# A hybrid decoder step on one core: norm and weight parts between the residual adds, down sums one group ahead, GpSimd issuing the down weights' transfers

## The reference, cut to what matters

```python
def out_and_mlp(x, a, b, w_out, g_mlp, w_up, w_down):
    x = x + jnp.concatenate([a, b], axis=-1) @ w_out
    hn = rmsnorm(x, g_mlp)
    return x + jnp.square(jax.nn.relu(hn @ w_up)) @ w_down

# per layer (one layer here), for x_prompt (1024 rows) and x_sample (8 x 8 rows), D_MODEL = 1024, D_FF = 4096
q, k, v, qi, ki, wi, bg, cg, h = project(rmsnorm(x, g_mix), w_in)
a = prompt_attention(...) or sample_attention(...)     # top-256 keys per query, 8 heads x 64
b, conv = conv_mixer(bg, cg, h, prev, conv_w)          # bg * conv3(cg * h), 512 channels
x = out_and_mlp(x, a, b, w_out, g_mlp, w_up, w_down)
y = rmsnorm(x, g_final)
```

## Time and profile before

| | us |
|---|---|
| median of 3 runs | 1790.15 (1788.7 to 1791.39) |
| the profiled execution, its time | 1778.85 |
| its span, first to last instruction | 1777.0 |
| PE busy | 1644.1, 93% |
| DVE busy | 997.3, 56% |
| ACT busy | 830.0, 47% |
| GpSimd busy | 628.2, 35% |
| mean granted PE clock | 0.955 of full speed |

### The profile page before, as it was taken

The page is one execution under the profiler, slowest core; times in us unless marked ns, Lnnn a source line. Parts: engine busy times, 40 slices in busy tenths (PEclk is TensorE's granted clock), DMA queues, the critical chain, the costliest instruction groups (busy, mean ns, idle before and its releaser), DMA issues.

```text
span 1777.0 us, 27949 instructions
## 1 busy us (share of the span) xinstructions
PE 1644.1 (93%) x10208; PEld 1267.5 (71%) x10208; DVE 997.3 (56%) x2212; ACT 830.0 (47%) x1597; POOL 628.2 (35%) x839
## 2 busy tenths in 40 slices
PE   8999999999888887778799879999999899999996
PEld 6653554999755565555579878888888788888885
DVE  5587889995634444444455764544444354444445
ACT  5565877775244444333353234444444353333334
POOL 1101325475645555544413214445445300400002
PEclk9999999999989989888999969999999999999998
DMA  8211320155867765554661136666666695455553
GB/s 242 52 48 52 119 68 36 46 173 174 268 206 222 218 191 162 156 154 135 185 168 36 36 112 208 217 222 205 218 224 224 222 337 166 162 188 172 163 172 134
DMA packets 153366, 288.47 MB, mean 162 GB/s; under 512 B 16971, under 2 KB 65471, under 8 KB 150930
## 3 DMA queue, kind: packets, MB, share of 16 engines
q1 hardware_dynamic: 131858, 214.97, 36.7%
q0 software_dynamic: 21376, 71.75, 13.5%
HBM read 215.18 MB, written 71.48 MB: 161 GB/s over the span
## 4 chain that ended last, share of the span: by engine, by line
PE 65%; issue 11%; DVE 8%; another core or an unknown queue 5%; ACT 5%; DMA 3%; POOL 2%; SPq 0%; DVEq 0%; POOLq 0%; ACTq 0%
PE psum L2407 6%; PE psum L2408 6%; PE psum L2409 6%; PE psum L2492 5%; PE psum L2494 5%; PE psum L2493 5%; PE psum L2235 2%; PE psum L2115 2%; PE psum L2257 2%; PE psum L1914 2%; PE psum L2144 2%; PE psum L1957 2%; PE psum L1958 1%; PE psum L1959 1%
## 5 line engine op out<-in xcount | busy, mean ns | idle before, releaser
L3269 DVE TENSOR_TENSOR ring_lo<-arena,ring_hi 128x1024 fp32r<-128x1024 f32 x112 | 141.3, 1264 | 159.5 <-ACT ring_hi L1653 159.3
L1653 ACT ACTIVATE ring_hi<-arena 128x1024 fp32r<-128x1024 f32 x112 | 118.6, 1060 | 194.2 <-DMA arena<-h_scratch 194.2
L2492 PE MATMUL psum<-ring_hi 128*128 128x512 f32 x448 | 176.7, 394 | 5.5 <-DVE ring_lo L3269 4.2
L2494 PE MATMUL psum<-ring_hi,ring_lo 128*128 128x512 f32 x448 | 175.5, 392 | 0.0
L2493 PE MATMUL psum<-ring_lo,ring_hi 128*128 128x512 f32 x448 | 175.0, 391 | 0.0
L1480 ACT ACTIVATE arena<-x_region,arena 128x384 bf16<-128x384 f32 (+2 forms) x192 | 166.5, 872 | 6.2 <-POOL arena L1192 6.2
L1227 POOL DMA_INDIRECT arena<-in_cache_v,arena x128 | 126.5, 988 | 112.6 <-PE psum L2216 79.4
L2630 DVE TENSOR_TENSOR wu_lo<-arena,wu_hi 128x512 fp32r<-128x512 f32 x112 | 83.7, 774 | 99.9 <-ACT wu_hi L1646 79.7
L1227 POOL DMA_INDIRECT arena<-in_cache_k,arena x96 | 96.4, 1004 | 100.8 <-PE psum L2115 77.2
L1545 ACT ACTIVATE arena<-psum 128x512 f32<-128x512 f32 (+3 forms) x64 | 33.2, 518 | 208.4 <-remote 104.2
L1646 ACT ACTIVATE wu_hi<-arena 128x512 fp32r<-128x512 f32 x112 | 67.9, 625 | 122.9 <-PE psum L2427 94.4
(11 more groups left out here) (429 smaller groups left out, 4081.3 us busy)
## 6 DMA issues: line engine op xcount, KB each, us to landing
h_scratch<-arena SPq DMA_DIRECT2D x112, 256.0 KB, 2.4
arena<-h_scratch SPq DMA_DIRECT2D x112, 256.0 KB, 3.6
arena<-in_w_down SPq DMA_DIRECT2D x16, 1024.0 KB
s_scratch<-arena SPq DMA_DIRECT2D x16, 1024.0 KB
arena<-s_scratch SPq DMA_DIRECT2D x64, 256.0 KB, 3.3
arena<-in_w_up SPq DMA_DIRECT2D x30, 512.0 KB, 4.4
arena<-in_w_down SPq DMA_DIRECT2D x48, 256.0 KB, 2.8
arena<-k_scratch SPq DMA_DIRECT2D x32, 256.0 KB
```

The costliest lines, as they stand in the source:

```text
L1653: act.activation(ring_hi[s % RING], ring_full[s % RING], ACT.Copy).then_inc(dn_high, 1)
L2492: pe.matmul(out, w_hi[:, col], h_hi, start=first, stop=False, skip_group_check=True)
L2494: ins = pe.matmul(out, w_lo[:, col], h_hi, start=False, stop=(k == NG - 1), skip_group_check=True)
L3269: dve.tensor_tensor(ring_lo[s % RING], ring_full[s % RING], ring_hi[s % RING], ALU.subtract).then_inc(dn_low, 1)
```

## The change

- DVE's `norm`, `low_early` and `low_late` are cut into pieces (`norm_root`, `norm_rows`, `norm_t3`, `norm_t2`, `norm_t1`, `low_n`, `low_t1`, `low_t2`, `low_t4`) that stand one behind each residual add u = 8 to 22, with the `up_low(0, i)` spread over u = 13 to 15. ACT's order follows: `norm_high(0)` ahead of the weight roundings.
- The third chunk's norm and parts are split in finer steps with more semaphore counts (`norm_high_last`, `low_last`), and its reciprocal and rows stand ahead of the first bank sums.
- In pass v = 1 the products go in the order 0, 4, 1, 2, 3, 5, 6, and sample half 0 follows product 2; in v = 0 `rms(2)` follows the second product.
- Sample half 0 uses one matmul of 256 columns for weights 0 and 2 together.
- `raw_down` and `sums_down` are issued by GpSimd. `down_sums(0)` comes before the group loop, and the sums of group g are made in the iteration that makes the up sums of group g, one group earlier than before.
- Ring slots 3, 4 and 5 lie in other places, and `fill(3)` to `fill(5)` stand before `h_sums`.
- The second halves of the last four row tiles are scaled by ACT instead of GpSimd.

```diff
-FIRST_NO = {i: n for n, i in enumerate((0, 2, 4, 1, 3, 5, 6))}
+UP_ORDER = {0: (0, 2, 4, 1, 3, 5, 6), 1: (0, 4, 1, 2, 3, 5, 6)}
...
+        wu_pair = at("wu_pair", w_at[0], 2048, F32R).rearrange("p (e x k c) -> p e x k c", e=2, x=2, k=4)
+        for e, i in enumerate((0, 2)):
+            wu_hi[i], wu_lo[i] = wu_pair[:, e, 0], wu_pair[:, e, 1]
...
-        ring_at = [RAWAT, WBLK, WBLK + 2048, WBLK + 4096, T4LO, T4HI]
+        ring_at = [RAWAT, WBLK, WBLK + 2048, T4LO, T4HI, WBLK + 4096]
...
@@ sync @@
-            raw_down(0)
             for g in range(NG):
...
-                    sums_down(g - 1)
-                    raw_down(g)
...
-                    sums_down(g)
                 h_second(v, g)
                 if g == NG - 1:
                     sp.wait_ge(up_done, up_no(v, 4))
                     fill(2)
+                    sp.wait_ge(up_done, 7 * len(VG))
+                    fill(3)
+                    sp.wait_ge(us_done, 2 * NG)
+                    fill(4)
+                    fill(5)
                 h_sums(v, g)
-            sp.wait_ge(us_done, 2 * NG)
-            fill(3)
-            sp.wait_ge(up_done, 7 * len(VG))
-            fill(4)
-            fill(5)
...
@@ gpsimd @@
+            def raw_down(k):
+                if k:
+                    pool.wait_ge(stg_out, STG_OUT0 + 16 * k)
+                pool.dma_start(stg, w_dn_v[:, 2 * k:2 * k + 2, :]).then_inc(stg_in, 16)
...
-            for g in range(NG):
-                if g + 1 < NG:
-                    for x in (1, 2, 3, 4):
-                        up_sum(g + 1, x)
-                    pool.wait_ge(w_low, weight_no(g + 1, 6))
+            pool.wait_ge(wo_ready, 3 * KT)
+            raw_down(0)
+            down_sums(0)
+            sums_down(0)
+            for g in range(1, NG):
+                for x in (1, 2, 3, 4):
+                    up_sum(g, x)
+                    if x == 1:
+                        raw_down(g)
+                pool.wait_ge(w_low, weight_no(g, 6))
                 down_sums(g)
+                sums_down(g)
...
-            for t in range(NB):
+            for t in range(NB // 2):
                 pool.wait_ge(row_scaled, ROW_SCALED0 + t + 1)
...
@@ scalar @@
             squares(1, 0, 4)
-            for i in (0, 2, 1, 4, 5, 3, 6):
+            norm_high(0)
+            squares(1, 4, 5)
+            for i in (0, 2, 1, 4):
                 up_high(0, i)
-            squares(1, 4, 5)
-            norm_high(0)
-            squares(1, 5, KT)
+            squares(1, 5, 6)
+            for i in (5, 3, 6):
+                up_high(0, i)
+            squares(1, 6, KT)
...
+            for t in range(NB // 2, NB):
+                act.wait_ge(row_scaled, ROW_SCALED0 + t + 1)
+                act.activation(yrow[t][:, 512:1024], yrow[t][:, 512:1024], ACT.Copy, scale=yroot[:, t:t + 1]).then_inc(y_rows_act, 1)
...
@@ tensor @@
+                    if half == 0:
+                        both = bank(7)[:, 0:2 * P].rearrange("p (e c) -> p e c", e=2)
+                        pe.matmul(both, n_pair[:, k, :], wu_pair[:, :, 0, k, :], start=(k == 0), stop=False, skip_group_check=True)
+                        ins = pe.matmul(both[0:SMP], n_pair[:, k, SMP:P], wu_pair[:, :, 1, k, :], start=False, stop=False, skip_group_check=True)
+                        continue
...
@@ vector @@
-                if u == KT + 1:
-                    norm(0)
-                if u == KT + 4:
-                    low_early(0)
-                if u == KT + 5:
-                    for i in (0, 2, 1, 4, 5, 3, 6):
-                        up_low(0, i)
...
+                if u == 8:
+                    norm_root(0)
+                if u == 9:
+                    norm_rows(0, 0, 6)
+                if u == 10:
+                    norm_rows(0, 6, KT)
+                    norm_t3(0)
+                    norm_t2(0)
+                if u == 11:
+                    norm_t1(0)
+                if u == 12:
+                    low_n(0)
+                if u == 13:
+                    low_t1(0)
+                    up_low(0, 0)
+                    up_low(0, 2)
...
+            norm_root(2)
+            norm_rows(2, 0, KT)
             first_sums(0)
             add_bank(0, 2, 4, h22, h22)
-            norm(2)
-            norm_t4(2)
-            dve.tensor_tensor(two_id, ident[:, 0:SMP], ident[:, SMP:P], ALU.add)
+            norm_t3(2)
+            norm_t2(2)
+            norm_t1(2)
             low_last()
```

More of the change, by code:

```diff
@@ L837, in up_no @@
         def up_no(v, i):
-            return 7 * v + (i if v else FIRST_NO[i]) + 1
+            return 7 * v + UP_ORDER.get(v, range(7)).index(i) + 1
         def weight_no(g, i):
@@ L1730, in _ @@
             h_from_bank(0)
-            norm_high(2)
+            norm_high_last()
             t4_high(2)
@@ L2393, in up_product @@
                 if v == 1:
[L2394 to L2395 removed]
+                    pe.wait_ge(n_low, {0: 5, 4: 5, 1: 6, 2: 6, 6: 9}.get(i, 7))
+                    if i == 4:
+                        pe.wait_ge(up_dve, 1)
+                    if i in (0, 4, 1, 2):
                         pe.wait_ge(wo_done, 3 * KT)
@@ L2418, in up_sample @@
                 if half and g == 0:
-                    pe.wait_ge(n_low, 8)
+                    pe.wait_ge(n_low, 10)
                 for k in range(4):
[L2421 to L2426, removed]
+                    if half == 0:
[3 more added lines that the diff above has]
+                        continue
+                    for e, w, s_pair in ((0, 3, n_pair[:, 4 + k, :]), (1, 6, sd_pair[:, k, :])):
+                        pe.matmul(bank(7)[:, e * P:(e + 1) * P], s_pair, wu_hi[w][:, k, :], start=False, stop=False, skip_group_check=True)
+                    for e, w, s_pair in ((0, 3, n_pair[:, 4 + k, :]), (1, 6, sd_pair[:, k, :])):
                         ins = pe.matmul(bank(7)[0:SMP, e * P:(e + 1) * P], s_pair[:, SMP:P], wu_lo[w][:, k, :],
-                                        start=False, stop=(half + k == 4), skip_group_check=True)
+                                        start=False, stop=(k == 3), skip_group_check=True)
                 ins.then_inc(us_done, 1)
@@ L2441, in _ @@
                 end = v == LASTV[g]
[L2442 to L2450, removed]
+                order = UP_ORDER.get(v, range(7))
+                for n, i in enumerate(order):
+                    up_product(v, i)
+                    if v == 0 and n == 1:
+                        rms(2)
+                    if g and n == 0:
                         turn_sample_h(g - 1)
-                    up_product(v, 1)
-                    up_product(v, 2)
-                    if end:
+                    if end and n == (3 if v == 1 else 2):
                         up_sample(g, 0)
-                    for i in (3, 4, 5, 6):
-                        up_product(v, i)
                 if end:
@@ L2555, in link, with norm_root, norm_rows, norm_t3 @@
                 dve.wait_ge(dve_step, steps[0] + steps[1])
-            def norm(c):
-                o, w = CH[c]
-                lo, hi = PAIRS[c]
+            def norm_root(c):
+                w = CH[c][1]
                 dve.wait_ge(root_ready, c + 1)
                 link(dve.reciprocal(root[:, 0:w], root[:, 0:w]))
-                for k in range(KT):
+            def norm_rows(c, first, last):
+                o, w = CH[c]
+                for k in range(first, last):
                     i = dve.scalar_tensor_tensor(out=n_full[:, k, o:o + w], in0=xT[:, k, o:o + w], scalar=colsT[:, KT + k:KT + k + 1],
                                                  in1=root[:, 0:w], op0=ALU.mult, op1=ALU.mult)
-                i.then_inc(norm_ready, 1)
-                dve.wait_ge(norm_ready, c + 1)
-                even, odd, into = halves(n_full, lo, hi, 0), halves(n_full, lo, hi, 1), halves(xT, lo, hi, 1)
-                link(dve.tensor_tensor(odd[:, 0:4], odd[:, 4:8], odd[:, 0:4], ALU.subtract))
-                dve.wait_ge(x_out, X_OUT0 + 16 * (c + 1))
-                link(dve.tensor_tensor(into[:, 4:8], odd[:, 0:4], even[:, 0:4], ALU.add))
-                dve.tensor_tensor(into[:, 0:4], odd[:, 4:8], into[:, 4:8], ALU.subtract).then_inc(n_made, 1)
+                if last == KT:
+                    i.then_inc(norm_ready, 1)
+            def norm_t3(c):
+                lo, hi = PAIRS[c]
+                odd = halves(n_full, lo, hi, 1)
+                dve.wait_ge(norm_ready, c + 1)
+                i = dve.tensor_tensor(odd[:, 0:4], odd[:, 4:8], odd[:, 0:4], ALU.subtract)
+                if c == 2:
+                    i.then_inc(n_made, 1)
+                    dve.wait_ge(n_made, 3)
+                else:
+                    link(i)
+            def norm_t2(c):
+                lo, hi = PAIRS[c]
+                dve.wait_ge(x_out, X_OUT0 + 16 * (c + 1))
+                link(dve.tensor_tensor(halves(xT, lo, hi, 1)[:, 4:8], halves(n_full, lo, hi, 1)[:, 0:4], halves(n_full, lo, hi, 0)[:, 0:4], ALU.add))
+            def norm_t1(c):
```

(3 more changed lines are left out.)

103 lines of the change are left out of this document (70 added, 33 removed).

## The result

The changed kernel takes 1809.35 us (1800.97 to 1815.0, 4 runs) where the kernel before took 1789.43 (1783.32 to 1791.39) beside it: ratio 1.0113, 95% interval 1.0064 to 1.0162. It is 20 us slower; 8.4 faster was forecast.

The account below looks back on a forecast made before the run. TensorE, busy 93%, bounds the kernel through its waits and half clock. 13.2 - 12.8 + 7.0 + 1.0 = 8.4 us off the median 1790.15 gives 1781.7 us; own range 1770 to 1793, eight in ten 1759 to 1803.

Parts of the forecast that it names:

- The place and the wait: Steady groups: up sum 2 waits in GpSimd's queue for the landed write, delaying ACT, DVE's bank sum and product 6; 2.0 us later.
- the sum of the round: Steady groups: 23.9 us a round against PE's 22.4, binding in 12 of 14 groups; stage 12.8 us longer, sample gain included.
- The round without meetings: Steady groups: bank sum to write 16.27, then 3.84, 0.54, 1.62 and 1.39 us, together 23.7 us a round.
- The meetings of DVE and GpSimd: Steady groups: up sum 3 takes turns with DVE's two low parts, adding 0 to 2 x 1.3 us; 0.2 taken.
- slower rival: Steady groups: DVE and GpSimd meet twice each round, 26.3 us a round, stage 41 us longer, 1810 us; chance 0.25.
- The first part: First residual add to v = 2: stall before the second root sum goes, v = 1 stays at half clock; gain 13.2 us.
- The meeting of DVE and the first down sums: Before v = 1: GpSimd's four first down sums lengthen DVE's chain by 0 to 5.2 us, 4.5 taken.
- The sample pairing: Sample half 0: eight matmuls of 256 columns for sixteen of 128 gain 0.37 us in each of 15 groups, 5.6 us.
- The start of the down products: First down products: earlier fills, last write and read out of SyncE's way, remove waits and half clock; gain 7.0 us.
- The last rows: End of kernel: ACT scales four of GpSimd's eight row halves; gain 1.0 us, 0 to 1.7.
- The clock holds: Rival: pass v = 1 keeps full clock, the rest as forecast, 1769.4 us; chance 0.13.

Follow-up runs that it names:

- the late read: Changed kernel with GpSimd issuing the read of the next down weights behind up sum 4 instead of up sum 1: 1746.36 us against 1776.38 before, ratio 0.9822.
- the run in which up sum 3 waits: Changed kernel with one wait added, up sum 3 starting only after DVE's low part of weight 1: 1778.57 us, ratio 1.0013 to the kernel before.
- the old scheme: Changed kernel with the down weights wholly as before (SyncE issues, down sums a group later), other edits kept: 1763.84 us against 1784.76 before, ratio 0.9875.

## Why the prediction was wrong, point by point

**The place and the wait: right.** Up sum 2 behind the wait for the landed write, ACT, DVE and the bank sum behind it, PE's product 6 last; the loop of five hand-overs; all of it is in the rows, and moving the read by one place removes it.

**The step that failed is the sum of the round, 23.9 us.** Two terms were mis-sized.

- *The round without meetings*, forecast at 23.7, measured at 24.53. From write to read 4.45 where 3.84 of SyncE's row was taken: 0.6. The sentence on the Trainium skill (DMA: Bandwidth & Descriptors, "Anatomy of one DMA — SWDGE (gpsimd) path") had 4.4, and this trace agrees: 4.43 and 4.45 from issue to the next instruction, the landing itself 4.2 behind the issue in the median. The read's issue 0.75 for 0.54: 0.2. Up sum 2 and the low parts 2.62 for 3.01: -0.4. The chain from bank sum to write 16.72 for 16.27: 0.45. Together 0.9. About 0.2 of it belongs to the added wait of the run that it is read from, so that 24.3 is nearer the truth.
- *The meetings of DVE and GpSimd*, forecast at 0.2, measured at 0.82 (one) and 1.87 (two). I had bounded them by 0 and 2.6 and put the value near the lower end, since a late PE would hold up sum 3 back. The rows show why it mostly doesn't: the wait moves up sum 2 so far back that product 4 is done when it ends, so up sum 3 follows at once (1251.40) and meets the low part of weight 2 in 11 of 13 rounds. A late PE holds back up sum 4 (0.47 us in the round from 1192.98, 0.21 in that from 1244.97), which is the difference between the two kinds of round. What I had counted on, a PE late enough to hold up sum 3, came in the two rounds behind 6.8 us of half clock, and there the low part of weight 1 took 1.79 instead.

Against PE's own 22.30 this makes 2.2 us a round and, on average, 1.2 more. Of the 14 rounds from the second write to the last, one takes 25.90 us on average in the changed kernel (1064.17 to 1426.82) and 22.47 in the late read: 48 us, where the forecast had 12 x 1.5 + 0.4 = 18.4. The stage: 335.2 + 47.3 = 382.5. By the run in which up sum 3 waits, 30.6 of the 47.3 are the queue's wait and 16.7 the meetings; with the 0.2 us a round that its own wait adds, nearer 28 and 19. So the slower rival's time (1810) came true, and its mechanism in part: its 26.3 us counted two meetings on 23.7; it is one or two meetings on 24.3 to 24.5.

**The first part: right, 12.7 for 13.2.** The stall ahead of the second root sum is gone with its half clock (1.00 from 980 to 1000), and from the first residual add to the first up product it is 93.5 us instead of 100.9, 7.4 less (7.0 forecast). From there to v = 1 it took 21.0 us, as forecast, but made up otherwise: PE waited 1.13 us at the root sum, for GpSimd's sum of squares, and 1.61 us before product 5, for the bank sums that stand behind the norm rows now (0 and 0 forecast), and 2.43 instead of 5.3 before v = 1. That these add up to the forecast is luck. The meeting of DVE and the first down sums was sized right: four operations took 4.1 us longer (1.68, 1.66, 2.29, 1.76), 4.5 forecast. The pass v = 1 took 23.1 us (22.3) at clock 0.51, with a wait of 1.16 us before product 6 that the forecast did not have.

**The sample pairing: right**, 0.45 for 0.37 a group; a matmul of 256 columns doesn't cost what two of 128 do. **The start of the down products: right in size** (6.7 for 7.0), and of the causes named the last write in SyncE's queue did most of it (5.6 of 8.7 us between the old scheme and the late read; the rest is open), the places of the fills nothing. **The last rows: right**, 1.0; that GpSimd's longer drain would else have cost 1.7 was not foreseen.

**The clock holds: refuted.** I had named two conditions, that the down sums miss DVE's chain and that PE's short waits don't cost the clock. With the first one given, the clock held for 8.5 us and then fell at a wait of 1.91 us for ACT, which half clock had hidden until then: the second condition failed.

## What to carry to other kernels

A DMA that waits for an earlier one to land belongs in the queue of an engine that has nothing urgent behind it, or behind the last urgent instruction; write down what follows it in the queue and where that engine waits anyway, since a wait that overlaps an existing one is free (0.85 us here) and the same wait one place earlier cost 47 us. When a wait moves an instruction, ask which others it now coincides with: a bound that looked unlikely in the old timing can become the rule in the new one (11 of 13 rounds here). A stall behind which a queue is already late is a loop: price the whole round, not the one delay.

## What the runs showed of the hardware

DVE's low parts, with both inputs in SBUF, took 1.7 us beside a GpSimd sum instead of 0.69 (that of weight 0, off the bounding chain, up to 2.3), while GpSimd's own took 1.29 and 1.47; DVE's bank sums, with one input in PSUM, kept their time beside GpSimd's sums. In the late read:

```profile
1217.26 1.29 POOL L1297 TENSOR_TENSOR arena<-arena 128x512 f32<-128x512 f32 x1
1218.62 1.28 POOL L1299 TENSOR_TENSOR arena<-arena 128x512 f32<-128x512 f32 x1
...
1218.06 0.69 DVE L3334 TENSOR_TENSOR arena<-psum,arena 128x512 f32<-128x512 f32 x1 [1.92 <-issue]
```

The Trainium skill (SBUF — State Buffer, "Who interferes with whom") says so too: with at most one SBUF input, outside its two-port modes, VectorE doesn't contend with GpSimd. The granted clock fell to half in the steady groups as well: in the second profile of the changed kernel for 3.4 to 6.8 us at six of its eight waits of 2.9 to 3.5 us, and at none of its four waits of 1.1 to 1.5. And GpSimd's closing drain ended 4.51 us behind its last work where it had issued the down weights' transfers, 1.89 where it had not.
